# Output stores and later input loads change queues, and one tile's statistics move, in an eight-core hybrid block

## The reference, cut to what matters

```python
def reference(x, norm1_g, w_in, conv_w, ..., norm2_g, w_up, w_down, final_g):
    h = rmsnorm(x, norm1_g[l])
    p = jnp.einsum('bsd,de->bse', h, w_in[l])          # B, C, x~ | u, v
    ...
    y_a = b_gate * causal_depthwise_conv(c_gate * xc, conv_w[l])
    v = layernorm(v, gmlp_ln_g[l], gmlp_ln_b[l])
    y_b = u * spatial_gating(v, gmlp_ws[l], gmlp_bs[l])
    y = jnp.concatenate([rmsnorm(y_a, ...), rmsnorm(y_b, ...)], axis=-1)
    x = x + jnp.einsum('bse,ed->bsd', y, w_out[l])
    h2 = rmsnorm(x, norm2_g[l])
    a = jax.nn.relu(jnp.einsum('bsd,df->bsf', h2, w_up[l]))
    x = x + jnp.einsum('bsf,fd->bsd', a * a, w_down[l])
    return rmsnorm(x, final_g)
```

## Time and profile before

| | |
|---|---|
| runs | 1243.12, 1238.66, 1243.27 us; median 1243.12 |
| profiled execution, its own time | 1242.04 us |
| its span, slowest core (core 1) | 1240.4 us; all cores 1226.6 to 1240.4 |
| TensorE busy on core 1 | 1196.5 us (96%), 6264 matmuls |
| VectorE, ScalarE, POOL busy | 942.2, 533.6 and 87.8 us |
| DMA | 253.86 MB, 205 GB/s on average |

### The profile page before, as it was taken

One profiled execution on the slowest core, in us unless ns is written; L12 is line 12 of the kernel. 1 busy time (PEld: TensorE's weight loads), 2 busy tenths in 40 slices (PEclk: granted clock), 3 DMA queues, 4 the chain that ended last, 5 costly groups with the idle time before them and its releaser, 6 DMA issues.

```text
span 1240.4 us, 19488 instructions; the slowest of 8 cores (1226.6 to 1240.4 us)
## 1 busy us (share of the span) xinstructions
PE 1196.5 (96%) x6264; PEld 586.0 (47%) x6264; DVE 942.2 (76%) x1460; ACT 533.6 (43%) x905; POOL 87.8 (7%) x148
## 2 busy tenths in 40 slices
PE   5899999999999999999999999999999999999994
PEld 3345646646556464444444444444444444444441
DVE  2799899989999897459879647768737867845745
ACT  4554664555644555036047016227205317404533
POOL 1100000000001001001101100101200000110000
PEclk8999999999999999999999999999999999999997
DMA  8968687696777959458897964666975655985424
GB/s 188 165 131 218 195 221 203 172 250 149 189 204 211 307 175 292 154 166 187 241 320 242 292 209 155 225 214 203 264 231 175 220 168 183 271 245 175 152 90 136
DMA packets 57011, 253.86 MB, mean 205 GB/s; under 512 B 6224, under 2 KB 8400, under 8 KB 56912
## 3 DMA queue, kind: packets, MB, share of 16 engines
q1 hardware_dynamic: 35152, 180.27, 44.0%
q0 software_dynamic: 21760, 72.36, 26.1%
HBM read 211.71 MB, written 65.01 MB: 223 GB/s over the span
## 4 chain that ended last, share of the span: by engine, by line
PE 87%; DMA 8%; DVE 2%; issue 1%; ACT 1%; SPq 0%; DVEq 0%; ACTq 0%; POOLq 0%
PE PS L506 87%; DMA RING_83<-ws_s 2%; DMA WSB_108<-wst 1%; DMA oT<-RA 1%; DMA RA<-x_s 1%; DMA WV<-wv 1%; DMA WCXB_51<-wcxb 1%; DMA X_75<-xT 1%; DMA WCXB_53<-wcxb 0%; DMA X_76<-xT 0%; DVE YN L522 0%; DVE RA L522 0%; SPq L533 0%; DVE RB L522 0%; DVE RA L525 0%
## 5 line engine op out<-in xcount | busy, mean ns | idle before, releaser
L522 DVE TENSOR_TENSOR RB<-PS,RB 128x512 f32<-128x512 f32 x128 | 88.4, 690 | 87.9 <-PE PS L506 84.7
L522 DVE TENSOR_TENSOR RA<-PS,RA 128x512 f32<-128x512 f32 x96 | 65.9, 689 | 65.6 <-PE PS L506 60.0
L506 PE MATMUL PS<-YN,WO 128*128 128x256 f16 x896 | 104.5, 273 | 3.2 <-ACT VH L513 1.9
L522 DVE TENSOR_TENSOR A_86<-A_86 128x512 bf16<-128x512 bf16 (+1 forms) x192 | 94.3, 508 | 11.8 <-ACT A_86 L513 7.5
L506 PEld LDWEIGHTS PS<-YN,WO 128*128 128x128 f16 x896 | 87.3, 98 | 22.0 <-issue 4.0
L513 ACT ACTIVATE SN_88<-PS 128x512 f32<-128x512 f32 x63 | 37.4, 596 | 100.8 <-PE PS L506 99.6
L506 PE MATMUL PS<-A_86,RING_82 128*128 128x512 bf16 x308 | 77.0, 382 | 3.3 <-DVE RB L522 3.3
L506 PE MATMUL PS<-A_86,RING_83 128*128 128x512 bf16 x308 | 77.3, 382 | 0.7 <-DMA RING_83<-ws_s 0.7
L506 PE MATMUL PS<-A_86,RING_81 128*128 128x512 bf16 x308 | 76.6, 379 | 0.0
L513 ACT ACTIVATE SN_89<-PS 128x512 f32<-128x512 f32 x63 | 37.3, 596 | 91.2 <-PE PS L506 91.1
L506 PE MATMUL PS<-A_86,RING_80 128*128 128x512 bf16 x308 | 76.4, 379 | 0.0
(11 more groups left out here) (236 smaller groups left out, 2090.1 us busy)
## 6 DMA issues: line engine op xcount, KB each, us to landing
RING_80<-ws_s SPq DMA_DIRECT2D x20, 896.0 KB, 6.4
RING_81<-ws_s SPq DMA_DIRECT2D x20, 896.0 KB, 6.9
RING_83<-ws_s SPq DMA_DIRECT2D x20, 896.0 KB, 7.2
RING_82<-ws_s SPq DMA_DIRECT2D x20, 896.0 KB, 5.7
RING_84<-ws_s SPq DMA_DIRECT2D x20, 896.0 KB, 6.4
RING_85<-ws_s SPq DMA_DIRECT2D x20, 896.0 KB, 6.7
ws_s<-PREP_70 SPq DMA_DIRECT2D x12, 896.0 KB, 6.6
ws_s<-PREP_69 SPq DMA_DIRECT2D x12, 896.0 KB, 9.3
```

Of the source, the lines that this page charges most:

```text
L506: ins = e.matmul(real(o_), lhsT=l, rhs=r, start=st, stop=sp, skip_group_check=True)
L522: dve(lambda e: e.tensor_tensor(out=out, in0=real(in0), in1=in1, op=op), reads, writes, n, rate, in0)
```

## The change

Four edits:

1. `schedule` makes 120 tries, not 60.
2. `stage_conv` returns the names of its three PSUM banks, and the statistics of the second tile (m = 1) also depend on those of the very first convolution, so that their matmuls on XQ_68 come after its 24 matmuls.
3. Loads of x from the fourth tile on (20 DMAs of 512 KB) are issued by POOL, through the software queue, not by SP.
4. All output stores are issued by SP. Those of the last group were there before; 24 of 512 KB change from POOL to SP.

The second argument of `dma`'s key only names the semaphore.

```diff
-    def schedule(self, phys, rounds=8, tries=60):
+    def schedule(self, phys, rounds=8, tries=120):
...
-        def stats(src, q, n, ones, rows=2, first=False):
+        def stats(src, q, n, ones, rows=2, first=False, behind=[]):
...
-                   q.keys(i, 2) + ONES)
+                   q.keys(i, 2) + ONES + behind)
...
-                dma("sp", b[:, 2 * j:2 * j + 2, :], src, after, b.keys(2 * j, 2) + landed, ("xl", (m + 1) % 3, j),
+                dma("sp" if m < 3 else "pool", b[:, 2 * j:2 * j + 2, :], src, after, b.keys(2 * j, 2) + landed,
+                    ("xl", m < 3, (m + 1) % 3, j),
                     4 * 128 * 2 * MT, key=first() if m < 3 else None, margin=0.5 if m < 2 else 4.0)
...
-        def stage0_stats(m):
-            return stats(X[(m + 1) % 3], XQ[m % 2], 8, ONESD, 8 if m < 2 else 2, m == 0)
+        def stage0_stats(m, behind=[]):
+            return stats(X[(m + 1) % 3], XQ[m % 2], 8, ONESD, 8 if m < 2 else 2, m == 0, behind)
...
             act(Z[:, c, 126:128], Z[:, c, 638:640], AF.Identity, Z.keys(c), Z.keys(c), n=2)
+            return bC.keys() + bX.keys() + bB.keys()
...
-                    dma("sp" if g == NGRP - 1 else "pool", oT[m].rearrange("p (k t) -> p k t", k=8)[:, j::4, :],
-                        b[:, j::4, :], bk, [("out", m, j)], ("os", g == NGRP - 1, h, j), 4 * 128 * 2 * MT)
+                    dma("sp", oT[m].rearrange("p (k t) -> p k t", k=8)[:, j::4, :],
+                        b[:, j::4, :], bk, [("out", m, j)], ("os", h, j), 4 * 128 * 2 * MT)
...
-        stage_conv(0, 0)
+        first_banks = stage_conv(0, 0)
...
-                        b0 = stage0_stats(1)
+                        b0 = stage0_stats(1, first_banks)
```

## The result

Four executions of the changed kernel took 1234.19 to 1236.32 us, median **1234.7**, beside 1243.19 for the kernel before on the same chip: a ratio of 0.9942, with a 95% interval of 0.9917 to 0.9967. So the change makes the kernel faster by some 0.4 to 0.6% (the intervals reach from 0.2 to 0.8%). The forecast was 1236.1, with 1231 to 1243. Every median and ratio here leaves out the executions in which some cores ran at a clearly lower granted clock, and four whole runs (after2, b_both, b_stores, b_x) on a chip where every core of every kernel, the one before too, ran at 0.82 to 0.89.

A forecast was written before the change was run, and what follows sets the result against it. TensorE's matmuls bound the kernel (87% of the chain), the slowest core setting the time. Core 1: 1240.4 - 1.3 - 1.0 - 4.9 = 1233.2; core 6 slowest at 1233.4, 1235.0 profiled, 1236.1 us median, range 1231 to 1243.

The forecast's parts named there:

- Second tile's stats: Front, first convolution: statistics matmuls on XQ_68 placed after its 24 matmuls, removing their 5.1 us wait from ahead; -1.3 us.
- they fit: Front: six more matmuls ahead of the bias matmul, 1.30 us, fit into its 2.90 us wait for WST.
- VH: Second tile's normalised v: fewer ScalarE squares ahead of it, more projection matmuls for TensorE; -1.0 of 1.9 us, all three cores.
- Stores on SP: Last group's opening: RB stall goes through VectorE's order and earlier store landing; -4.9 us core 1, -4.5 core 0, -2.6 core 6.
- the 8.7 us taken for SP: Last group's opening: RA's 512 KB store takes 8.7 us on SP, 4.1 sooner than 12.81 on POOL.
- The add of RB: Last group's opening, VectorE: two fewer multiplies between the first and second add of RB, worth 1.33 us.
- x loads on POOL: Fourth tile on: twenty x loads leave SP for POOL, some 7 us of delay costing nothing; cost 0.
- More tries: Whole program: 60 to 120 scheduler tries re-draw the order everywhere; unpriced, put into the range as 1 us either way.
- The stall stays: Rival: transfers bound by bytes, not queue, so only the front's 2.3 us gained on core 1; 1240.8 us, chance 0.30.
- Stores behind ring loads: Rival: on SP, ring loads go ahead of stores, which land later; +9.2 us on core 1, 1252.3 us, chance 0.09.
- The front gives all: Rival: the whole 5.1 us XQ_68 wait is won, since loads follow sooner; 1230 to 1233.5 us, chance 0.13.
- a start well before 58 us: Sign for the rival of a fully won front: the bias matmul, at 59.97 us on core 1, starting that early.

The follow-up runs named there:

- after2: The changed kernel measured again, first try of after3; left out because the chip ran every kernel at 0.82 to 0.89 clock, so no time is given.
- b_both: The changed kernel's order with both queues as before, first try of b_both2; left out for the chip's low clock, no time given.
- b_stores: The changed kernel's order kept, only the 24 output stores put back on POOL; left out for the chip's low clock, no verdict, not repeated.
- b_x: The changed kernel's order kept, only the 20 later x loads put back on SP; left out for the chip's low clock, no verdict, not repeated.
- tries120: The control: the kernel before with 120 scheduler tries in place of 60, order came out row for row the same; 1245.7 us, ratio 1.0020.
- fix_vh: The kernel before with one ScalarE activation moved: the last square of XQ_67 goes behind the second tile's VH; 1240.6 us, ratio 0.9995.
- f_both: The kernel before, its order kept, with output stores on SP and later x loads on POOL together; 1240.9 us, ratio 0.9963.
- f_x: The kernel before, its order kept, with only the 20 later x loads issued by POOL; 1240.1 us, ratio 0.9985.
- b_both2: The changed kernel's order with both queues as before (stores of groups 0 to 2 on POOL, x loads on SP); 1236.9 us beside 1240.9, ratio 0.9969.
- after3: Second measurement of the changed kernel, nothing altered; 1235.4 us beside 1240.0 for the kernel before, ratio 0.9962.
- f_stores: The kernel before, its order kept, with only the 24 output stores issued by SP; 1241.5 us, ratio 0.9985.

## Why the prediction was right in its number and mostly wrong in its reasons

**Second tile's stats (taken as -1.3 us).** Not found. The idle time of the first 62 us is 15.4 to 16.2 in the old order and 15.2 to 16.2 in the new one. TensorE's timeline of the changed kernel on core 0 shows the wait in its new place, and the bias matmul no sooner; a row of the chain of waits on that core names the load behind it.

```profile
22.36 3.57 PE L506 MATMUL PS<-HT_65,WCXB_51 128*128 128x512 f16 x8 [4.52 <-DVE WCXB_51 L529]
...
33.99 2.75 PE L506 MATMUL PS<-HT_65,WCXB_52 128*128 128x512 f16 x12 [2.07 <-DVE WCXB_52 L529]
...
60.54 0.41 PE L506 MATMUL PS<-WST,ONE_46 128*64 128x128 f16 x8 [1.37 <-DVE Z L522]
```

```profile
12.18 9.39 DMA WCXB_51<-wcxb
```

The step that failed is "they fit": the matmuls placed ahead of the bias matmul were to fill the wait for WST, but two waits, on WCXB_51 and WCXB_52, had been left out of the sum. I had taken the XQ_68 wait as the thing that held the convolution; behind it stood the load and the scaling of the convolution's own weights, hidden by it. On the mean of the eight cores, TensorE's waits for XQ tiles in the first 62 us fell from 11.8 to 8.5 us and those for WST from 1.0 to none, while those for WCXB tiles rose from 0.7 to 6.1. The count was off as well: by TensorE's timeline four matmuls more stand ahead of the bias matmul, not six (134, not 136), since four of HT_66 with WCXB_51 moved behind it and two of WCXB_53 ahead; at the pace of the earlier trace rows that is 0.9 us and not 1.3. And not even that is sure: the bias matmul starts, on the mean of the cores, at 56.4 to 56.8 us in four executions of the old order (before, tries120, fix_vh, f_both) and at 57.2, 57.8 and 59.1 in the three of the new one.

**VH (taken as -1.0).** Right in place and cause, a little small: 1.9 to 0.6 on every core, 1.3 us, of which fix_vh shows 0.7 for the square on ScalarE.

**Stores on SP (taken as -4.9 on core 1, -4.5 on core 0, -2.6 on core 6).** This step failed, and it was the largest. It took the landing of one store, 12.81 us, for that of the queue, and one execution's stall for a property of the kernel. The median landing on core 1 of the 24 stores that moved, before and after:

```profile
oT<-RA POOLq DMA_DIRECT2D x12, 512.0 KB, 8.2
oT<-RB POOLq DMA_DIRECT2D x12, 512.0 KB, 9.9
```

```profile
oT<-RA SPq DMA_DIRECT2D x12, 512.0 KB, 8.9
oT<-RB SPq DMA_DIRECT2D x12, 512.0 KB, 8.5
```

So the 8.7 us taken for SP was right, but POOL's stores landed in as little: there were no 4.1 us to win. Averaged over the eight cores these medians are 9.6, 9.9 and 9.8 us on POOL in the old order (before, tries120, f_x), 10.1 on SP in the same order (f_both), and in the new order 9.6 on POOL and 9.0 and 8.7 on SP (b_both2; after, after3). In the old order the queue brings nothing; in the new one it may bring 0.6 to 0.9 us, which so few executions do not settle. The add of RB is earlier in VectorE's order, as predicted. But the stall that this was to remove came and went in the old order too: I read it from one execution's slowest core and took it off in full. The control, with the same order, has no such wait on core 1 and 4.2 us on core 6; a core's mean is 0.7 to 1.5 us in three executions of the old order on the old queues, and that is about the most that the edit could give an average core. The move of the stores alone measured 0.9985.

**x loads on POOL (taken as 0).** Right. Nor do they land much later, 9.6 to 12.4 us on core 1 in the median; the same twenty loads took 9.4 to 11.5 from SP before:

```profile
X_75<-xT POOLq DMA_DIRECT2D x8, 512.0 KB, 12.4
X_76<-xT POOLq DMA_DIRECT2D x8, 512.0 KB, 9.6
...
X_74<-xT POOLq DMA_DIRECT2D x4, 512.0 KB, 9.8
```

Averaged over the eight cores these medians are 9.7 to 10.0 us from SP (before, tries120, b_both2) and 10.0 to 10.6 from POOL (f_x, f_both, after, after3). The changed kernel issues the first load of the fourth tile at 95.40, 12 us sooner than in the earlier trace rows (on core 1 all is sooner by then: the first square of it stands at 115.71, not 124.67), and the idle time from 110 to 400 us does not grow (1.5 and 1.4).

```profile
95.40 0.53 POOL L533 DMA_DIRECT2D X_75<-xT  x1 [14.20 <-DMA x_s<-X_75]
```

The Trainium skill, "SBUF — State Buffer", warns in its box on DMAs from GpSimd's queue that their descriptors may have to wait for VectorE. The issue took 0.53 us in this row, as it did for all twenty of these loads on core 1, and the landings are later by some 0.3 us on average; so little of such a wait is seen, and no run here separates it from the rest of the traffic.

**More tries (taken as 1 us either way, unpriced).** The tries themselves did nothing to the old program. But the new order that came with the other edits was the cause of most of the gain, and I had no term for it. Most of it lies in the passage at 400 to 600 us, where the idle time of before has two parts of about 1.0 us a core each. The first is a wait on VectorE, 0.8 to 1.6 us on every core: one sum of H_93 stands behind a sum of SQ_62. TensorE and VectorE in before, on core 1:

```profile
432.68 1.02 PE L506 MATMUL PS<-H_93,RING_80 128*128 128x512 f16 x4 [0.82 <-DVE H_93 L522]
```

```profile
429.65 0.68 DVE L522 TENSOR_TENSOR SQ_62<-SQ_62 128x1024 bf16<-128x1024 bf16 x1
430.25 2.28 DVE L522 TENSOR_TENSOR H_93<-H_93 128x4096 f16<-128x4096 f16 x1
```

In the changed kernel the sum of H_93 stands ahead of that of SQ_62, and TensorE comes to it with no wait, on any core:

```profile
424.43 1.02 PE L506 MATMUL PS<-H_93,RING_80 128*128 128x512 f16 x4
```

```profile
421.90 2.28 DVE L522 TENSOR_TENSOR H_93<-H_93 128x4096 f16<-128x4096 f16 x1
424.10 0.69 DVE L522 TENSOR_TENSOR SQ_62<-SQ_62 128x1024 bf16<-128x1024 bf16 x1
```

The second part is a wait for weights from the ring. In before, on core 1, the load of RING_83 is issued behind that of RING_84 and a store of rs_s on SP, and behind four residual loads on POOL, the first of them shown; SP, then POOL:

```profile
470.61 0.32 SPq L533 DMA_DIRECT2D RING_84<-ws_s  x1
471.25 1.04 SPq L533 DMA_DIRECT2D rs_s<-RS_78  x1
472.48 0.91 SPq L533 DMA_DIRECT2D RING_83<-ws_s  x1
```

```profile
465.96 0.72 POOL L533 DMA_DIRECT2D RA<-x_s  x1 [34.61 <-PE PS L506]
```

and RING_83, which TensorE waits for at 492.86, is 20.2 us under way. In the changed kernel RING_83 is issued at 458.93, ahead of RING_84 and the store, the four residual loads had begun at 451.96, and it takes 10.7; TensorE has no wait there on any core. The issues of that stretch on core 1, before and after:

```profile
RING_83<-ws_s SPq DMA_DIRECT2D x1, 896.0 KB, 20.2
```

```profile
RING_83<-ws_s SPq DMA_DIRECT2D x1, 896.0 KB, 10.7
```

Neither of these loads is one that the change moved, and b_both2 has nearly the same idle time there with the old queues (0.3 us, 0.1 in the changed kernel). On core 6 the two rows of TensorE that waited for it in before were

```profile
492.85 2.75 PE L506 MATMUL PS<-A_86,RING_83 128*128 128x512 bf16 x12 [1.63 <-DMA RING_83<-ws_s]
498.38 1.02 PE L506 MATMUL PS<-A_86,RING_85 128*128 128x512 bf16 x4 [1.91 <-DMA RING_85<-ws_s]
```

and I had seen them only as part of a core that was not the slowest. Yet the page of the kernel before had named this load, as the largest transfer in the chain of the earlier trace rows:

```profile
PE PS L506 87%; DMA RING_83<-ws_s 2%; DMA WSB_108<-wst 1%; DMA oT<-RA 1%; DMA RA<-x_s 1%; DMA WV<-wv 1%; DMA WCXB_51<-wcxb 1%; DMA X_75<-xT 1%; DMA WCXB_53<-wcxb 0%; DMA X_76<-xT 0%; DVE YN L522 0%; DVE RA L522 0%; SPq L533 0%; DVE RB L522 0%; DVE RA L525 0%
```

That the earlier sum and the earlier load are what ended the two waits is read from the timelines; neither was tried by itself.

**The sum.** 1236.1 was forecast, 1234.7 measured. The agreement is partly luck: 7.2 us were taken off core 1 for reasons of which 1.3 us, those of VH, are sure on an average core, and an average core gained some 2 us more (1.9 to 2.3) in a stretch that the sum did not touch. The mean of the eight spans fell by some 2.4 to 3.2 us (1232.8 to 1230.4 in the last call; 1233.25 to 1230.05 in the two profiled executions). The slowest core, which sets the time, gained more in the first measurement than in the second (8.5 and 4.6 us between the medians).

**The rivals.** "The stall stays" was right about the mechanism, in that the change of queue by itself did nearly nothing for an average core; this is the rule of the Trainium skill, "DMA: Bandwidth & Descriptors", section "Issuing engines are not separate DMA queues", and runs f_stores (0.9985) and b_both2 beside after3 (0.9969 and 0.9962) agree with it within their intervals, while f_both (0.9963) leaves a part that it does not explain. It was wrong about the time, since it had the new order as noise of both signs. "Stores behind ring loads" did not come: the waits on RING tiles fell. "The front gives all" did not come either: the mean start of the bias matmul did not fall. The sign for it, a start well before 58 us, was drawn from core 1's 59.97 alone; core 1 had 55.40 after the change, and the cores of the kernel before already differed from 52.8 to 59.97.

What stays open: which of the edits led the scheduler to the new order (that it was the dependency in front, the changed engines or their costs was not tried), and how much the queues add in the new order, and why the slowest core lies nearer to the mean of the eight with both of them moved.

## What to carry to other kernels

A wait that one execution shows on one core, or a landing read from one transfer, is not a term of a sum until a second execution, or the other seven cores, show it too; add the idle time up over the cores and stretches first. Where a scheduler orders the program, an edit can re-draw the whole order, and the draw can be worth as much as the edit (here -0.3% in one case and +0.5% in another): test an edit in the frozen old order, and the new order without the edit, before crediting either. Before counting a removed wait, look for what stands behind it: here the weights of the same convolution. And go through the chain of waits link by link: here its largest transfer was the load that the new order moved.

## What the runs showed that I had not expected

The second part's RB wait moves between cores by chance: in two executions of the same order core 1 had 3.3 us and none, core 6 2.6 and 4.2, while the eight cores' mean was 1.5 in both. A program whose time is its slowest core of eight therefore moves from one execution to the next by more than such a wait: the mean of the spans of the kernel before was 1232.8 to 1234.2 us in three calls, its slowest core 7.0 to 7.5 above that, and single executions of one call took from 1237.4 to 1251.1 us.
